# Two ends of a two-layer encoder: the first two weight chunks interleaved by depth pairs, and 256 columns of the last norm's first pass on ScalarE and GpSimd

## The reference, cut to what matters

```python
def layer_norm(x, g, b):
    x32 = x.astype(jnp.float32)
    mu = jnp.mean(x32, axis=-1, keepdims=True)
    var = jnp.mean(jnp.square(x32 - mu), axis=-1, keepdims=True)
    y = (x32 - mu) * lax.rsqrt(var + LN_EPS) * g.astype(jnp.float32) + b.astype(jnp.float32)
    return y.astype(x.dtype)

def swiglu_ffn(x, w_up, w_down):
    gate, up = jnp.split(x @ w_up, 2, axis=-1)
    return (jax.nn.silu(gate) * up) @ w_down

for l in range(DEPTH):     # DEPTH = 2
    x = layer_norm(ALPHA * x + 0.5 * swiglu_ffn(x, ffn1_w_up[l], ffn1_w_down[l]), ln1_g[l], ln1_b[l])
    mix = hybrid_mixer(x, w_in[l], ...)
    x = layer_norm(ALPHA * x + mix, ln2_g[l], ln2_b[l])
    x = layer_norm(ALPHA * x + 0.5 * swiglu_ffn(x, ffn2_w_up[l], ffn2_w_down[l]), ln3_g[l], ln3_b[l])
```

## Time and profile before

| | us |
|---|---|
| median of 3 runs | 1100.02 |
| lowest and highest of them | 1099.73, 1100.76 |
| the profiled execution | 1100.38 |
| its span (first to last instruction) | 1098.5 |
| PE busy | 1090.3 |
| DVE busy | 796.9 |
| ACT busy | 590.5 |
| GpSimd busy | 367.8 |

### The profile page before, as it was taken

One profiled execution on the slowest core, in us unless ns is written; L12 is line 12 of the kernel. 1 busy time (PEld: TensorE's weight loads), 2 busy tenths in 40 slices (PEclk: granted clock), 3 DMA queues, 4 the chain that ended last, 5 costly groups with the idle time before them and its releaser, 6 DMA issues.

```text
span 1098.5 us, 18341 instructions
## 1 busy us (share of the span) xinstructions
PE 1090.3 (99%) x6377; PEld 926.5 (84%) x6377; DVE 796.9 (73%) x1102; ACT 590.5 (54%) x850; POOL 367.8 (33%) x441
## 2 busy tenths in 40 slices
PE   9999999999999999999999999999999999999997
PEld 8888888998788888888888888889877888888886
DVE  6686866789878867686677566477897787656644
ACT  6565533574873556463345555336858645645530
POOL 3998971108700289993200000011284000000000
PEclk9999999999999999999999999999999999999999
DMA  9876673743665595667466666636545666666641
GB/s 288 263 228 225 232 232 114 230 119 128 175 214 192 178 291 180 190 216 239 130 209 192 206 211 205 210 90 210 168 132 158 202 200 215 193 204 210 208 161 39
DMA packets 159551, 211.09 MB, mean 192 GB/s; under 512 B 12952, under 2 KB 107640, under 8 KB 159488
## 3 DMA queue, kind: packets, MB, share of 16 engines
q1 hardware_dynamic: 155360, 202.56, 58.5%
q10 hardware_dynamic: 2688, 3.44, 1.3%
q0 software_dynamic: 1440, 4.27, 1.2%
HBM read 209.11 MB, written 1.10 MB: 191 GB/s over the span
## 4 chain that ended last, share of the span: by engine, by line
PE 99%; DVE 0%; DVEq 0%; issue 0%
PE ps L846 24%; PE ps L788 17%; PE ps L789 17%; PE ps L790 17%; PE ps L850 12%; PE ps L1185 2%; PE ps L1187 1%; PE ps L1188 1%; PE ps L859 1%; PE ps L802 1%; PE ps L1053 1%; PE ps L1071 1%; PE ps L1100 1%; PE ps L1121 1%; PE ps L1111 1%; PE ps L1279 0%
## 5 line engine op out<-in xcount | busy, mean ns | idle before, releaser
L1307 DVE TENSOR_TENSOR wlo<-raw,whi 128x1024 fp32r<-128x1024 f32 (+1 forms) x367 | 478.6, 1330 | 121.3 <-ACT whi L450 118.4
L450 ACT CAST whi<-raw 128x1024 fp32r<-128x1024 f32 (+1 forms) x367 | 377.2, 1042 | 233.2 <-PE ps L790 157.2
L846 PE MATMUL ps<-x_hl,whi 128*128 128x512 f32 x1152 | 362.5, 396 | 0.1
L850 PEld LDWEIGHTS ps<-x_hl,wlo 128*128 128x128 f32 x1152 | 216.4, 188 | 51.1
L850 PE MATMUL ps<-x_hl,wlo 128*128 128x256 f32 x1152 | 226.5, 278 | 0.0
L1770 POOL TENSOR_TENSOR rstd<-var_eps,cst 128x1 f32<-128x1 f32 x11 | 16.8, 1528 | 531.0 <-DVE var_eps L1375 531.0
L846 PEld LDWEIGHTS ps<-x_hl,whi 128*128 128x128 f32 x1152 | 175.7, 189 | 0.6 <-issue 0.3
L788 PE MATMUL ps<-whi,x_hl 128*128 128x512 f32 (+1 forms) x400 | 156.6, 392 | 0.0
L789 PE MATMUL ps<-wlo,x_hl 128*128 128x512 f32 (+1 forms) x400 | 153.1, 383 | 0.0
L790 PE MATMUL ps<-whi,x_hl 128*128 128x512 f32 (+1 forms) x400 | 153.1, 383 | 0.0
L788 PE MATMUL ps<-whi,hh 128*128 128x512 f32 (+1 forms) x355 | 138.0, 389 | 0.0
(11 more groups left out here) (203 smaller groups left out, 1357.8 us busy)
## 6 DMA issues: line engine op xcount, KB each, us to landing
raw<-in_ffn_w_up SPq DMA_DIRECT2D x352, 256.0 KB, 3.9
raw<-in_ffn_w_down SPq DMA_DIRECT2D x176, 256.0 KB, 3.3
raw<-in_w_in SPq DMA_DIRECT2D x128, 256.0 KB, 3.5
raw<-in_w_branch SPq DMA_DIRECT2D x32, 256.0 KB, 3.3
raw<-in_w_out SPq DMA_DIRECT2D x32, 256.0 KB, 3.7
bias_g<-bias_rows ACTq DMA_DIRECT2D x16, 192.0 KB, 3.9
raw<-in_w_in SPq DMA_DIRECT2D x16, 148.0 KB, 2.3
affine<-in_ln_g SPq DMA_DIRECT2D x4, 512.0 KB, 5.7
```

The costliest lines, as they stand in the source:

```text
L450: nc.scalar.copy(whi[:, s % RING, 0:w], raw[:, s % RAW, 0:w]).then_inc(S["hi_done"], 1)
L846: nc.tensor.matmul(ps[:, bank, :], w(whi, s + q, at, at + P), x_hl[:, k, :, :], start=k == 0, stop=False)
L850: ins = nc.tensor.matmul(ps[:, bank, 0:SEQ], w(wlo, s + q, at, at + P), xh[:, k, :], start=False, stop=k == KT - 1)
L1307: nc.vector.tensor_tensor(wlo[:, s % RING, 0:w], raw[:, s % RAW, 0:w], f32(whi[:, s % RING, 0:w]), ALU.subtract).then_inc(S["split_done"], 1)
```

## The change

**Opening.** The tiles are numbered anew: tile s = 2d + c holds the pair of depths 2d, 2d+1 of chunk c, so that the two chunks alternate: 0, 1, 0, 1. SP loads in this order (`load_opening`), with the x columns of pair d ahead of tile 2d; tiles 0 to 3 come by halves, tiles 4 to 7 whole. ACT and DVE split in this order. PE takes tiles 0 to 3 in the order of kinds (both token tiles for each of the three products) and tiles 4 to 7 by token. Chunk 0 is complete in tile 6, chunk 1 in tile 7. ACT's and DVE's queues change behind tile 7: the casts and subtractions of tiles 8 to 11 stand ahead of chunk 0's silu and h, where they stood behind. The wait for chunk 0's second token tile is now for tile 6 (`used(7)`).

**Tail.** ACT adds epsilon as bias of the root and reads the variance itself; DVE's addition goes. The first pass of columns 768 to 1023 leaves DVE: ACT computes mean - x there, GpSimd multiplies by the negated gain (`neg_gain`, made by ACT behind row tile 0's root), and DVE's second piece of the last pass waits for it (`end_ready`). On DVE the first pass of columns 512 to 767 stays.

```diff
+END_DVE = 768
...
+    neg_gain = b_t[:, 0, 0:2, :].rearrange("p a b -> p (a b)")
...
         if t == 0:
             eng.wait_ge(S["up_done"], by_tokens(f, c) + 1)
         else:
-            eng.wait_ge(S["pe_used"], used(s + 4))
+            eng.wait_ge(S["pe_used"], used(7) if f == 0 and c == 0 else used(s + 4))
...
+            def load_opening(w):
+                for s in range(2 * RAW):
+                    d, c = s // 2, s % 2
+                    if c == 0 and d > 0:
+                        load_columns(d)
+                    if s < RAW:
+                        for k, landed in ((2 * d, half_landed[s]), (2 * d + 1, raw_landed[s])):
+                            dst = raw[:, s, depth(k)].rearrange("p (g n) -> p g n", g=2)
+                            sp.dma_start(dst, w[0, :, k, :, c, :]).then_inc(landed, 16)
+                    else:
+                        dst = raw[:, s % RAW, :].rearrange("p (t g n) -> p t g n", t=2, g=2)
+                        load(0, s, [(dst[:, :, g], w[0, :, 2 * d:2 * d + 2, g, c, :]) for g in range(2)])
+                sp.dma_start(ident[:, :], A["ident"]).then_inc(S["ident_landed"], 16)
...
             def token_chunk(f, s, c):
-                if f == 0 and c == 1:
-                    split_hi(0, s + RING)
+                if f == 0:
+                    for q in range(4 if c == 0 else 1):
+                        split_hi(0, s + RING + q)
                 for t in range(NT):
                     wait_up(act, f, s, c, t)
...
                     if t == (1 if f == 0 else 0):
-                        for q in range(1 if f == 0 and c == 1 else 0, 4):
+                        for q in range((4 if c == 0 else 1) if f == 0 else 0, 4):
                             split_hi(0, s + RING + q)
...
             act.wait_ge(S["var_ready"], 6 * DEPTH - 1)
             nc.scalar.activation(std[:, 0:1], var_eps[:, 0, :], ACT.Sqrt)
+            act.wait_ge(S["affine_landed"], 32 * 3 * DEPTH)
+            nc.scalar.mul(neg_gain, affine[:, 0, END_DVE:D], -1.0).then_inc(S["centre_ready"], 1)
             act.wait_ge(S["var_ready"], 6 * DEPTH)
-            nc.scalar.activation(std[:, 1:2], var_eps[:, 1, :], ACT.Sqrt).then_inc(S["std_ready"], 1)
+            nc.scalar.activation(std[:, 1:2], mean_var[:, 1, 1:2], ACT.Sqrt, bias=cst[:, 15:16]
+                                 ).then_inc(S["std_ready"], 1)
+            nc.scalar.activation(x[:, 1, END_DVE:D], x[:, 1, END_DVE:D], ACT.Identity, bias=mean_var[:, 1, 0:1],
+                                 scale=-1.0).then_inc(S["centre_ready"], 1)
...
+                for s in range(2 * RAW):
+                    for k in (s // 2 * 2, s // 2 * 2 + 1):
+                        ins = by_kind(s, k) if s < RAW else by_token(s, k)
+                    ins.then_inc(S["pe_used"], 1)
...
-                link(nc.vector.bn_aggr(mean_var[:, 1, :], end_stats[:, :, :].rearrange("p a b -> p (a b)")))
-                nc.vector.tensor_scalar_add(var_eps[:, 1, :], mean_var[:, 1, 1:2], LN_EPS
-                                            ).then_inc(S["var_ready"], 1)
+                nc.vector.bn_aggr(mean_var[:, 1, :], end_stats[:, :, :].rearrange("p a b -> p (a b)")
+                                  ).then_inc(S["var_ready"], 1)
+                dve.wait_ge(S["var_ready"], 6 * DEPTH)
...
-                link(centred(512, 1024))
+                link(centred(512, END_DVE))
                 for a, b in END_PIECES:
+                    if b == D:
+                        dve.wait_ge(S["end_ready"], 1)
...
+            pool.wait_ge(S["centre_ready"], 2)
+            nc.gpsimd.tensor_tensor(x[:, 1, END_DVE:D], x[:, 1, END_DVE:D], neg_gain, ALU.mult
+                                    ).then_inc(S["end_ready"], 1)
```

More of the change, by code:

```diff
@@ L378, in ffn @@
                 for c in range(PEEL):
[L379 to L388, removed]
+                    if n == 0 and c < OLD_C:
+                        if c == 0:
+                            load_opening(w_up)
                     else:
@@ L759, in _ @@
                 act.dma_start(x_cols[:, k, :], A["x_t"][0, :, k, :]).then_inc(cols_landed[k], 16)
[L760 to L770, removed]
+            for s in range(RAW):
+                for k in (s // 2 * 2, s // 2 * 2 + 1):
+                    if s % 2 == 0:
+                        columns_hi(k)
+                    if k % 2 == 0:
+                        act.wait_ge(half_landed[s], 16)
+                        nc.scalar.copy(whi[:, s, depth(k)], raw[:, s, depth(k)]).then_inc(S["half_hi"], 1)
+                    else:
+                        act.wait_ge(raw_landed[s], 16)
+                        nc.scalar.copy(whi[:, s, depth(k)], raw[:, s, depth(k)]).then_inc(S["hi_done"], 1)
+            for s in range(RAW, 2 * RAW):
+                if s % 2 == 0:
+                    columns_hi(s)
+                    columns_hi(s + 1)
+                split_hi(0, s)
             for l in range(DEPTH):
@@ L856, in opening, with product @@
             def opening():
[L858 to L862, removed]
+                def product(a, ring, s, k, t, stop=False):
+                    return nc.tensor.matmul(ps[:, 2 * (s % 2) + t, :], a[:, k, tok(t)], ring[:, s, depth(k)],
+                                            start=k == 0 and a is xh and ring is whi, stop=stop)
@@ L863, in wait_hi @@
+                def wait_hi(s, k):
                     if k % 2 == 0:
-                        pe.wait_ge(S["half_hi"], k // 2 + 1)
+                        pe.wait_ge(S["half_hi"], s + 1)
                     else:
[L866 to L870, removed]
-                    else:
[L872 to L876, removed]
+                        pe.wait_ge(S["hi_done"], s + 1)
@@ L890, in opening @@
[L890 to L902, removed]
@@ L904, in opening @@
-                for k in range(2):
-                    wait_lo(KT + k)
-                    for t in range(NT):
[L907 to L916, removed]
-                            ins.then_inc(S["up_done"], 1)
+                        ins = product(xh, wlo, s, k, t)
@@ new lines, in by_kind, with by_token @@
+                    return ins
+                def by_token(s, k):
+                    if s % 2 == 0:
+                        pe.wait_ge(S["cols_lo"], k + 1)
+                    wait_lo(s, k)
+                    for t in range(NT):
+                        product(xh, whi, s, k, t)
+                        product(xl, whi, s, k, t)
+                        ins = product(xh, wlo, s, k, t, stop=k == KT - 1)
+                        if t == 0 and k == KT - 1:
+                            ins.then_inc(S["up_done"], 1)
+                    return ins
@@ L1328, in token_chunk @@
             def token_chunk(f, s, c):
-                if f == 0 and c == 1:
-                    split_lo(0, s + RING)
+                if f == 0:
+                    for q in range(4 if c == 0 else 1):
+                        split_lo(0, s + RING + q)
                 for t in range(NT):
```

53 lines of the change are left out of this document (28 added, 25 removed).

## The result

The changed kernel takes 1104.41 us (median of 6 runs, 1103.71 to 1105.70) against 1100.37 (6 runs, 1099.73 to 1100.76): the ratio is 1.0039, 95% interval 1.0028 to 1.0049. It is slower, by 4.0 us. The forecast was 1103.0, +3.0 over the 1100.02 that the kernel before had then, with a range of 1101.5 to 1105.1. Over three more runs of the kernel before its median moved to 1100.37.

What follows compares the result with a forecast made beforehand. PE's own stream was taken to bound the kernel, with only the opening and the tail able to move the time. +2.9 us (opening) and +0.1 (tail) on 1100.02 gave 1103.0 us, range 1101.5 to 1105.1.

Steps and rivals of the forecast that it cites:

- a wait ahead of PE counts in full: Whole span: PE is busy 99%, so no later idle time of PE could swallow a wait put in front of it.
- What the interleaving can win: Opening, chunks 0 and 1: a gain of 0.35 us at the most, taken as 0.05.
- The stall: Ahead of chunk 2: silus queue behind tile 11's cast, so chunk 2 starts at 30.3, not 27.43; +2.9 us.
- the 1478 ns issue: Tile 11's load: if one slow issue recurs, it lands near 26.9; if not, 25.8; 26.7 taken.
- Rival A: Behind the wait ahead of chunk 2: the clock falls, PE loses 1 to 2.1 us more; 1104.7 us, chance 0.25.
- The tail at +0.1: After the last matmul: clean savings of 0.35 us against 0.47 us that GpSimd's multiply takes from DVE.
- the sum that followed it to the letter: Tail: by the exclusive-lock rule DVE would lose up to 0.62 us, making the tail +0.27 and not +0.1.
- B: Opening: no stall at all, tile 11 landing by 23.7; 1099.4 us with the clean tail, chance 0.08.
- C: Opening and tail: tile 11 lands at 25.8 and the tail is clean; 1101.7 us, chance 0.12.

Runs made afterwards that it cites:

- without the stall: The changed kernel with chunk 0's silus between the splits of tiles 9 and 10 and the tail of before: 1100.21 us, ratio 1.0002.
- Kept busy: The changed kernel with ten more warm-up matmuls at the end of the opening: 1103.18 us, ratio 1.0028.
- one column: The kernel before with the changed tail, but GpSimd multiplies 1 column and not 256: 1100.09 us in one run.
- casts first: The kernel before with only the splits of tiles 8 to 11 moved ahead of chunk 0's silus and h: 1103.87 us, ratio 1.0031.
- opening alone: The changed kernel with the four edits of the tail undone: 1104.29 us, ratio 1.0041.
- three casts: The changed kernel with chunk 0's silus and h between the splits of tiles 10 and 11: 1102.02 us, ratio 1.0021.

## Why the prediction came out as it did

- **What bounds the kernel; a wait ahead of PE counts in full.** Right. 2.8 us of wait at 27.5 are 2.8 us at the end; the table's last column shows that nothing later swallowed them. The kernel before did have a second small wait, 0.28 us of PE's weight load at 50.9, too short for the view of waits that the prediction read.
- **What the interleaving can win: 0.05 of at most 0.35.** Not contradicted: the ratio is 1.0002 without the stall, but the interval of 1 us can't tell 0.05 from 0.35. The traces show no gain either, with chunk 2 at 27.39 and 27.70 where the old opening has 27.43, 27.91 and 27.88. What it left out is that the new order also has a wait of its own in some executions (tile 1's load is now needed first); the wait for its cast shows in two of the six profiles with this opening, 0.55 and 0.3 us. Two more have 0.3 and 0.7 us ahead of the very first group, which stands in the same place as before. None of it can be told in the times.
- **The stall.** Right in place, cause and size. Tile 11 was to land at 26.7 and its cast began at 26.62; chunk 2 was to start at 30.3 and started at 30.26. The way there was less exact: the 1478 ns issue did not recur (the longest issue of those loads was 472 ns), and the second half then should have landed at 25.8. It landed just before 26.6, because it was issued at 21.84 and took 4.8 us, just above the highest landing time of the earlier trace rows and not at their median. Two errors met, which is luck; the bounds, 25.8 and 27.1, were wide enough for either.
- **Rival A, the clock.** This is the term that was mis-sized: the sum has nothing for the clock, and the fall stood as a rival with a chance of 0.25 and 1.7 us. It came in at least five of the six runs of the change, and it cost 1.5 us in the profiled one. Kept busy, the kernel is 0.9 to 1.2 us faster in the median. Of the 1.4 us between 1103.0 and 1104.41, 0.35 are the new median of the kernel before, and the rest, 4.0 for 3.0 us, is of the size of the clock's share. The measured time lies beyond the forecast's own spread, which ended at 1103.8, and inside rival A's 1104.0 to 1105.1; the stated range held it because it took rival A in. The reason that was given against it, that the wait is hardly longer than the 2.8 us after the last matmul, was no reason: a length that sufficed once can suffice again.
- **The tail at +0.1.** It is 0.0. The clean savings were 0.08 and 0.26 as worked out; DVE's loss was 0.34 and not 0.47. GpSimd began at 1097.73, just behind DVE's centring of 1097.70, seems to have stood behind it, and then held up the last pass. It took 1.02 us, where the earlier trace rows have 0.62 for this width, and where a multiply that reads two full operands, as this one does, took 0.74 in the kernel before. Shown is that the 256 columns cost DVE the 0.34 us (one column gave them back). That each engine was held up by the instruction of the other that had started earlier is read from the order of the starts; the single column's 0.48 us beside a centring of 0.47 fits it. The rule in the Trainium skill, "SBUF — State Buffer", on the shared port pair as an exclusive lock fits this order of events; the sum that followed it to the letter, +0.27, was too high, since DVE lost 0.34 and not 0.62.
- **Rivals B and C.** B fell with the casts first: the queue's order makes the stall even where chunk 0 is ready 11 us early. C's landing of tile 11 at 25.8 was not seen in any execution; the earliest is 26.3, in the one with one column.

## What to carry to other kernels

A queue is in order: before work is moved ahead of a short instruction that the bottleneck waits for, look at what that work itself waits for. Here the casts of two tiles that had yet to land stood ahead of the silus, and these two positions in ScalarE's queue were worth 4 us. A wait of TensorE can cost more than its length: behind waits of 2.4 and 2.8 us here the clock was halved for 3.4 us, at a cost of 1.5 us, and work that kept TensorE busy in the wait took this away. And what is handed from VectorE to GpSimd has to be charged with what GpSimd then takes from VectorE: here 0.34 us, all that the edits saved.

## What the runs showed of the hardware

The length of PE's idle time alone did not decide whether the clock fell. In the change PE was idle from 27.5 and the clock fell at 29.95, and with the casts first it was idle from 27.8 and the clock fell at 30.47, in both cases before or shortly after work came back; with the opening alone PE was idle for about 3.0 us and the clock stayed, and with three casts for 2.3 us, likewise. What decides it is open. It differs between executions of one and the same kernel: the mean clocks above show it in at least five of six runs of the change and two of ten with three casts, and in none of eight with PE kept busy. Nor was it expected that the cast of one and the same tile would move by more than 1 us between executions (tile 10's: 25.23 in the change, 26.65 with three casts). Of these 1.4 us, 0.6 came from a later issue of its second half (20.33 and 20.91), and 0.8 from a longer way to its landing (4.9 and 5.7 us).
